# One-column products widened to 128 columns, and products of constants in TensorE's waits, in a two-block transformer kernel

## What is computed

```
    for i in range(DEPTH_2):
        sh1, sc1, g1, sh2, sc2, g2 = jnp.split((silu_c @ ada_w[i] + ada_b[i])[:, None, :], 6, axis=-1)
        hx = modulate(xs, sh1, sc1)
...
        xs = layer_norm(alpha * xs + g1 * yx, ln_g[i, 0], ln_b[i, 0])
        hx = modulate(xs, sh2, sc2)
...
            fx = peer(hx.reshape(-1, d), peer_wq[i], peer_keys[i], peer_u[i], peer_v[i]).reshape(bsz, s_len, d)
        xs = layer_norm(alpha * xs + g2 * fx, ln_g[i, 1], ln_b[i, 1])
```

## Time and profile before

| what | value |
|---|---|
| median of 3 runs (lowest, highest) | 2336.67 us (2336.33, 2339.16) |
| the profiled execution's own time | 2336.15 us |
| its span | 2334.8 us |
| PE busy | 2261.0 us, 97% of the span |
| DVE busy | 1866.3 us, 80% |
| ACT busy | 1186.1 us, 51% |
| mean granted TensorE clock | 0.987 of 2.4 GHz |

### The profile page before, as it was taken

How to read it: one execution, slowest core, us unless ns; L and a number is a source line. 1 busy time by engine, 2 the same in 40 slices (tenths; PEclk the granted TensorE clock), 3 DMA queues, 4 the chain that set the end, 5 groups by cost and what they waited for, 6 DMA issues and landing times.

```text
span 2334.8 us, 34700 instructions
## 1 busy us (share of the span) xinstructions
PE 2261.0 (97%) x13406; PEld 1889.3 (81%) x13406; DVE 1866.3 (80%) x3388; ACT 1186.1 (51%) x1753; POOL 169.3 (7%) x75
## 2 busy tenths in 40 slices
PE   7999999999999999999999998899999999999997
PEld 6789987776788888887777877788888888777786
DVE  7679987468779988888888887769998888887656
ACT  6555654347455555554444454445565554444443
POOL 0000000000034410000000000014430000000000
PEclk9999999999999999999999999999999999999999
DMA  7456684233556555545558895355555555556663
GB/s 284 132 178 199 214 325 142 79 99 100 174 170 197 182 181 172 173 166 177 172 171 326 327 343 195 129 198 188 185 188 169 175 169 171 171 172 243 207 213 121
DMA packets 123363, 442.31 MB, mean 189 GB/s; under 512 B 13744, under 2 KB 16816, under 8 KB 122560
## 3 DMA queue, kind: packets, MB, share of 16 engines
q1 hardware_dynamic: 117320, 425.04, 53.6%
q10 hardware_dynamic: 5880, 15.06, 1.9%
HBM read 436.88 MB, written 3.16 MB: 188 GB/s over the span
## 4 chain that ended last, share of the span: by engine, by line
PE 81%; DVE 12%; ACT 4%; issue 2%; DMA 1%; SPq 0%; ACTq 0%; DVEq 0%
PE psum L430 20%; PE psum L438 14%; PE psum L439 14%; PE psum L440 14%; PE psum L431 10%; PE psum L433 3%; DVE spl L2478 3%; PE psum L2741 3%; PE psum L432 1%; DVE cv L2008 1%; ACT spl L1039 1%; DVE acc L1683 1%; ACT cv L1334 1%; PE psum L2682 1%; DVE sm L2153 1%
## 5 line engine op out<-in xcount | busy, mean ns | idle before, releaser
L2478 DVE TENSOR_TENSOR spl<-ring,spl 128x1024 fp32r<-128x1024 f32 x639 | 783.4, 1227 | 358.8 <-ACT spl L1039 356.9
L1039 ACT ACTIVATE spl<-ring 128x1024 fp32r<-128x1024 f32 x703 | 738.7, 1053 | 473.7 <-PE psum L433 352.9
L430 PE MATMUL psum<-hT,spl 128*128 128x512 f32 x2016 | 728.6, 400 | 2.6 <-DVE hT L1663 2.3
L431 PE MATMUL psum<-hT,spl 128*128 128x256 f32 x2016 | 565.6, 281 | 0.0
L430 PEld LDWEIGHTS psum<-hT,spl 128*128 128x128 f32 x2016 | 380.8, 189 | 81.0 <-issue 2.9
L438 PE MATMUL psum<-spl,Ws 128*128 128x512 f32 x1024 | 411.5, 402 | 1.0 <-DVE Ws L2516 0.7
L439 PE MATMUL psum<-spl,Ws 128*128 128x512 f32 x1024 | 404.5, 395 | 0.0
L440 PE MATMUL psum<-spl,Ws 128*128 128x512 f32 x1024 | 403.9, 394 | 0.0
L431 PEld LDWEIGHTS psum<-hT,spl 128*128 128x128 f32 x2016 | 382.4, 190 | 9.5
L1613 ACT ACTIVATE Ws<-S 128x256 fp32r<-128x256 f32 x256 | 106.9, 419 | 384.9 <-PE psum L440 379.9
L2798 POOL TENSOR_TENSOR spl<-ring,spl 128x1024 fp32r<-128x1024 f32 x64 | 162.9, 2545 | 1173.7 <-ACT spl L1039 1173.7
(11 more groups left out here) (397 smaller groups left out, 2997.7 us busy)
## 6 DMA issues: line engine op xcount, KB each, us to landing
ring<-in_peer_u SPq DMA_DIRECT2D x256, 512.0 KB, 3.8
ring<-in_peer_v SPq DMA_DIRECT2D x256, 512.0 KB, 3.6
vring<-in_ada_w SPq DMA_DIRECT2D x56, 512.0 KB, 6.1
ring<-in_w_up SPq DMA_DIRECT2D x44, 512.0 KB, 4.5
aring<-in_ada_w SPq DMA_DIRECT2D x40, 512.0 KB, 6.1
ring<-in_ab_in SPq DMA_DIRECT2D x32, 512.0 KB, 3.5
ring<-in_peer_wq SPq DMA_DIRECT2D x32, 512.0 KB, 4.5
ring<-in_w_down SPq DMA_DIRECT2D x22, 512.0 KB, 5.9
```

Source lines behind the costliest of these rows:

```text
L430: q.matmul(b[:, :].rearrange("p (z t) -> p z t", z=2), l[0], r, start=start, stop=False)
L431: return q.matmul(b[:, 0:256], l[1], r[:, 0], start=False, stop=False)
L1039: q.activation(P.spl[:, m % SPLITS, 0, 0:w], P.ring[:, m % SLOTS, 0:w], ACT.Copy).then_inc(*P.hi.mark(m))
L2478: q.tensor_tensor(P.spl[:, n % SPLITS, 1, 0:w], P.ring[:, n % SLOTS, 0:w], P.spl[:, n % SPLITS, 0, 0:w].bitcast(F32), ALU.subtract).then_i ...
```

## The change

There are four edits.

1. The eight (or sixteen) one-column products of a sum become products of 128 columns. Each writes its column and 127 more behind it, which the next product overwrites. The right columns are left.
2. A new helper, `pe_warm`, issues n products of the identity with a matrix of ones, 128 columns each, into a free bank. Nobody reads them. It is called with 28 at the start, ahead of the first tile.
3. `pe_turns` calls it with 18 between the transposes of tb 0 and those of tb 1. It is used five times: at the heads of `up`, `ab`, `peer0`, `pool` and `peer1`. At `up` the third bank no longer waits for the first sum to be copied out (`fold_out(P, 0)`), only the fourth does.
4. Two sums, 9 and 10, move from `v_end` to slots between tiles of the second table of `peer0` (behind tiles 115 and 124), and with them the DVE copies.

```diff
-    folds += [("v", 0, places[8 * i + 7][2] + 3) for i in range(5, 9)] + [("v_end",), ("v_end",), ("v", 1, 84)]
+    folds += [("v", 0, places[8 * i + 7][2] + (3 if i < 10 else 2)) for i in range(5, 11)] + [("v", 1, 84)]
...
+def pe_warm(q, P, bank, n):
+
+    for _ in range(n):
+        q.matmul(P.ps[bank][:, 0:128], P.ident[:, :], P.ones[:, :], start=True, stop=True)
...
-                    t = q.matmul(banks[0][:, 8 * z + m:8 * z + m + 1],
+                    t = q.matmul(banks[0][:, 8 * z + m:8 * z + m + 128],
                                  acc[:, z if ada_two(i) else ada_half(i), m * 128:(m + 1) * 128],
-                                 P.ones[:, 0:1], start=True, stop=True)
+                                 P.ones[:, :], start=True, stop=True)
...
+    pe_warm(q, P, 7, 28)
...
+def pe_turns(q, P, pe, banks, src, first, spare, free):
+
+
+    for tb in range(2):
+        if tb:
+            q.wait_ge(*free)
+            pe_warm(q, P, spare, 18)
+        for k in range(8):
+            b = P.ps[banks[k // 2]]
+            if tb == 0 and k % 2 == 0:
+                q.wait_ge(*first[k // 2])
+            if k % 4 == 0:
+                q.wait_ge(*src(k, tb)[1])
+            o = k % 2 * 256 + tb * 128
+            t = q.transpose(b[:, o:o + 128], src(k, tb)[0], P.ident[:, :])
+            if tb and k % 2:
+                t.then_inc(*pe.mark(("turn", k // 2)))
...
-    pe_turns(q, P, pe, None, (2, 3, 6, 7), 8,
+    pe_turns(q, P, pe, (2, 3, 6, 7),
              lambda k, tb: (P.hn[:, tb, k * 128:(k + 1) * 128], (dve if k // 4 else act).at(("hn", tb, k // 4))),
-             wdve.at(("lo", 1)), wdve.at(("lo", 3)), fold_out(P, 0), fold_out(P, 0))
+             (wdve.at(("lo", 1)), wdve.at(("lo", 3)), wdve.at(("lo", 5)), fold_out(P, 0)), 0, wdve.at(("x1", 0, 0)))
...
-    pe_fold(q, P, ("v_end",))
-    pe_turns(q, P, pe, None, (0, 1, 2, 3), 8,
+    pe_turns(q, P, pe, (0, 1, 2, 3),
              lambda k, tb: (P.xr[:, tb, k * 128:(k + 1) * 128], ln_out(vact, vdve, tb, k // 4)),
-             fold_out(P, 9), fold_out(P, 10), vdve.at(("us", 63)), vdve.at("gates1"))
+             (fold_out(P, 9), fold_out(P, 10), vdve.at(("us", 63)), vdve.at("gates1")), 4, vdve.at(("y", 0, 0)))
...
-    dve_folds(q, P, dve, (1, 0))
-    dve_ada(q, P, ("v_end",))
-    dve_folds(q, P, dve, (1, 1))
+    dve_folds(q, P, dve, (1, 0), (1, 1))
```

More of the change, by code:

```diff
@@ L793, in pe_ab @@
     pe, act, dve = P.stage("ab")
-    pe_turns(q, P, pe, None, (4, 5, 6, 7), 8,
+    pe_turns(q, P, pe, (4, 5, 6, 7),
              lambda k, tb: (P.xr[:, tb, k * 128:(k + 1) * 128], (ddve if k // 4 else dact).at(("xn", tb, k // 4))),
-             ddve.at(("x2", 0, 0)), ddve.at(("x2", 0, 1)), ddve.at(("x2", 1, 0)), fold_out(P, 2))
+             (ddve.at(("x2", 0, 0)), ddve.at(("x2", 0, 1)), ddve.at(("x2", 1, 0)), fold_out(P, 2)), 2,
+             P.stage("up")[2].at(("conv", 18)))
     for i, c in enumerate(AB_CHUNK):
@@ L2659, in pe_peer @@
         first = [b4dve.at(("mTf", 2)), b4dve.at(("mTf", 3)), b4act.at(("e", 5)), b4act.at(("e", 7))]
-    pe_turns(q, P, pe, None, (0, 1, 2, 3), 8,
-             lambda k, tb: (P.xr[:, tb, k * 128:(k + 1) * 128], ln_out(b4act, b4dve, tb, k // 4)), *first)
+    pe_turns(q, P, pe, (0, 1, 2, 3),
+             lambda k, tb: (P.xr[:, tb, k * 128:(k + 1) * 128], ln_out(b4act, b4dve, tb, k // 4)), first, 4,
+             b4dve.at(("y", 0, 0)))
     for f in range(16):
```

## The result

The changed kernel takes 2341.12 us (median of 18 runs, 2336.81 to 2344.11), against 2336.5 us for the kernel before (18 runs beside them). The ratio is **1.0018, 95% interval 1.0012 to 1.0025**: slower by 4.6 us, just inside the 0.2% that I had called no change, and the interval reaches over that bound. The forecast was 2341.4.

A forecast was written before the change was run, and what follows sets the result against it. The prediction took PE to bound the kernel (81% of the chain); 0 + 2.6 + 1.1 - 1.7 + 0.45 + 0.5 + 0.75 + 1.5 = +5.2 on 2336.15 gave 2341.4 us, range 2335.5 to 2345.5.

The forecast's parts named there:

- Pass cost (112 ns): In every block: a 128-column float32 pass costs 112 ns at full speed, so 18 products (36 passes) take 4.03 us.
- rival (c): Blocks shorter than the waits, a repeated pass costing under 70 ns: not slower, +0.3, 2336.5; chance 0.12.
- Start (0): First tiles: the block ends at 9.8 and the third tile is held by DVE's split until 16.23, so 0.0.
- Rival (b): Slower through the start if the clock rises after 9.5: at most +1.9, 2343.3; chance 0.10.
- `up` (+2.6 and +1.1 for the clock): Head of `up`: the block behind the wait delays PE's second tile by 2.6; half speed behind that wait adds 1.1.
- Second sum (-1.7): Behind the second sum, at 292: the widened sum keeps the clock, -1.7.
- `ab`, `peer0`, `peer1` (+0.45, +0.5, +0.75): Those three heads: blocks outlast their waits by 1.26, 0.87 and 0.98, less what full speed gives back.
- Moved sums (+3.2): Second table of `peer0`: two 16-pass sums where PE has no pause cost 3.6, less the last tile's 0.34 wait.
- Head of `pool` (-1.7): Without the sums ahead, the block is covered and the first bank is ready at 1436.2, not 1438.1: -1.7.
- rival (a): The clock falls again behind the blocks: +1.0 at `up`, +0.8 at `ab`, +0.35 at `peer0`, 2343.5; chance 0.06.

The follow-up runs named there:

- after again: The changed kernel, unchanged, run and profiled a second time: 2340.17 us, ratio 1.0018 against the kernel before.
- 45 at the start: The changed kernel with 45 products in place of 28 in the block at the start: 2342.87 us, ratio 1.0030 against the kernel before.
- 36 at `peer`: The changed kernel with 36 products in place of 18 in the blocks at `peer0` and `peer1`: 2349.42 us, ratio 1.0059 against the kernel before.
- the block inside the wait at `up`: The changed kernel with the block at `up` put ahead of the transposes that wait for the first sum's copy: 2337.49 us, ratio 1.0004 against before.

## Why the prediction was right, step by step

- **Pass cost (112 ns).** Right: 36 passes end 4.02 later at `ab`, and the doubled blocks gave 8.04 for 72. This is the number on which the sum rests, and rival (c) falls with it.
- **Start (0).** Right: block over near 10.3 (9.8 predicted), since the clock rose 5.0 us after the block's start and not 4.2; the third tile was still held by DVE. Rival (b) needed a rise after 9.5; it came at 6.7. The -0.6 in the table is `xr`, which landed 0.6 earlier.
- **`up` (+2.6 and +1.1 for the clock).** The first term is the upper end of what came: 1.85 to 2.6 in the three executions whose clock stayed full in the block (after again, 45 at the start, 36 at `peer`). The second is not one number: in the profiled execution of after it was the full 1.6 (5.81 us for 36 passes), in the other three 0. Both ends were in the bounds, but over the four executions `up` costs 2.5 and not 3.7.
- **Second sum (-1.7).** Right: -1.5 in both profiles of after and with the wide sums alone.
- **`ab`, `peer0`, `peer1` (+0.45, +0.5, +0.75).** Right: 0.6, 0.6 and 0.7.
- **Moved sums (+3.2).** Right: 3.0, and PE has no idle time ahead of them.
- **Head of `pool` (-1.7).** This is the term that was mis-sized. The working, a bank ready earlier, gave 1.2 to 1.3 in four executions. In the two of the changed kernel itself the head gave 2.8 and 2.9, since the half-speed stretch of 1446.1 came before the second tile. I had not counted that stretch at all. My list of half-speed stretches was not complete: the profile before has others at 26.2, 480.1, 562.1 and 1446.1. Two of them bear on the sum:

```profile
480.20:483.40 3.20, 3.08 (x11) 0.50 0.02 5
1446.20:1449.40 3.20, 3.20 (x9) 0.50 0.70 218
```

- **The attention of `ab` (0).** Missing from the sum: before has half speed from 480.1 to 483.5, about from the end of a wait of PE for DVE on (1.46 us, to 480.32); it is gone (-1.5) in eight of the twelve profiles of edited kernels, among them both of the changed kernel, though nothing near it was edited. It stays in those of the wide sums only, the moved sums only, no block at `up` and the block inside the wait at `up`. No edit separates the two sets, so I take it for a question of where PE's pause falls in time; that is argued, not shown.
- **Two more that I had as 0.** Ahead of the moved sums +1.0 arises. It is a drift on `peer0`'s first table: from 843 to 1035 us every tile takes 3.080 us instead of 3.063, where nothing was edited. All twelve profiles of edited kernels have this drift (1.0 to 1.1), neither of before does; the wide sums alone and the moved sums alone both have it and share no edit that runs there. But `peer1`'s first table can have the same drift (1.0, from 1757 to 1941 us), and there the unchanged kernel has it in its second profile and not in its first, and the changed kernel likewise. So the table can go at either pace with no edit at all; what sets the pace stays open. Behind `peer1`'s head the two profiles of after lose 0.8 and 1.0, but not at one place: the second by this drift, the first in one step at 2150, at the first tiles of the second table. Eight other profiles of edited kernels have a step there (0.3 to 1.2), neither of before has, and its cause stays open too.

So in the profiled execution the terms of the mechanism came out within 0.3 but for the head of `pool` (-1.1), and with the attention (-1.5) and the start (-0.6) this is partly cancelled by the +1.8 outside the heads. The medians (+4.6) are nearer to the forecast (+4.7 on the median) than the profiles are, which took 1.2 and 2.5 us less than the medians of their runs; what a median execution has that these two lack, no trace shows. The direction and most terms came from the working; that the sum came out within 0.1 of the medians is luck, since two misses of 1.1 and 1.5 one way met 1.8 the other way.

On the clock: behind the block at `ab` PE does eight transposes (1.04 us), waits 0.89 and goes on at full speed, so rival (a) falls there, and at `up` and `peer1` too. The Trainium skill, "TensorE: Matmul & The Clock Gate", Part 4, holds that transposes don't count as PE being busy in the same way; the trace's rows don't say whether these transposes run in the mode that it speaks of. At `ab` and `peer1` transposes and a pause behind the block did not end the full speed in any of the six executions with a block of 18 or 36 there. At `peer0` they did in three of the six (no block at `up`, block inside the wait, 36 at `peer`), 1.5 to 2 us after the first product's start, and it cost nothing that shows (0.5 to 0.6 in the two with 18 products, as in the changed kernel). At `pool` (transposes and then 1.6 us idle) half speed followed in all six, with the first tile or with the second:

```profile
610.50:613.70 3.20, 3.20 (x10) 0.50 0.00 0
```

(`peer0`, no block at `up`.) These rows don't decide between transposes and idle time as its cause.

What was wrong in the picture as a whole was not a number: I gave the blocks the credit for the clock at `up` and `pool`. The wide sums alone shorten the half speed there (from 10.2 to 3.4 us at `up`, from 10.2 to 6.8 at `pool`), at no cost; in time that gave 0.55 to 1.0 at `up` and 0.0 to 1.6 at `pool`.

## What to carry to other kernels

Filler work for the clock belongs inside the wait and must be shorter than the wait: here 2.5 us in a wait of 2.6 was worth 0.65 us at best, 4.0 us in the same wait lost 0.6, and the same block behind a wait lost 1.85 to 3.5. Before adding filler, widen what is there: a product with 1 column that takes as long as one with 128 (106 and 112 ns a pass here) is a free place to do work that kept the clock in these runs. And look where half speed lies: 6.7 us of it at `peer0`, where DVE paces PE, gave back only 0.3 when it went, while 3.4 us behind the second sum, where PE had no pause, gave 1.5.

## What the runs showed of the hardware that I had not expected

- 22 float32 passes take 2.51 us with 1 column and 2.62 with 128, but only with 128 was the clock 1.00 behind them (0.50 with 1 column), with the same order of PE's instructions. The same for sums of 32 passes: 0.50 behind them before, 1.00 after.
- The granted clock of one and the same PE sequence isn't one and the same: the block at `up` took 4.18 us in three executions and 5.81 in a fourth, and the half-speed stretch behind the block at `pool` began with the first tile in two executions and with the second in four, 1.6 us apart in cost. A single profile can't price such a place.
- The transfer of `xr` took between 7.9 and 9.8 us from its issue to ACT's first use of it. With its issue (10.7 to 11.9) this puts its landing between 18.6 and 20.9, and the offset of the sixth tile is the difference in landing, to 0.1 us, in all fourteen profiles: everything behind the start moves by up to 2.3 us.
- One and the same table went at 3.063 or 3.080 us a tile in two profiles of one kernel, for some sixty tiles on end.
